# The triangular inverses of a delta-rule layer, moved from 64x64 units to compact 32x32 diagonal blocks with one corner step

## The chip, the core and the metric

One core of a Trainium2 chip runs one program that computes a four-layer network on 256 tokens of width 1024. The metric is the device time of one execution in microseconds, taken as the median of several runs. The engines are TensorE (PE, with its weight loads shown apart as PEld), VectorE (DVE), ScalarE (ACT), GpSimd (POOL) and the DMA queue of SyncE (SP). TensorE writes only to PSUM, which has eight banks of 512 float32 columns. VectorE and ScalarE carry results from PSUM to SBUF. VectorE also has a transpose that turns each 32x32 block of a tile in its place.

## What is computed

The network has an RG-LRU layer, a sparse attention layer, an RWKV-7 layer and a differential attention layer, each followed by a squared-ReLU MLP. The change touches only the recurrence of the third one:

```python
def _wkv7_scan(r, decay, k, v, a_in, b_in):
    def step(S, inp):
        r_t, w_t, k_t, v_t, a_t, b_t = inp
        sa = jnp.einsum('bhij,bhj->bhi', S, a_t)
        S = (S * w_t[:, :, None, :] + sa[..., None] * b_t[:, :, None, :]
             + v_t[..., None] * k_t[:, :, None, :])
        y_t = jnp.einsum('bhij,bhj->bhi', S, r_t)
        return S, y_t
```

There are 16 heads of width 64 and 256 tokens. The kernel cuts the tokens into four chunks of 64. Within a chunk the term with `sa` makes each token depend on the earlier ones, which is a triangular system: for each head and chunk it needs the inverse of a 64x64 matrix I - N, where N is strictly triangular. That is 16 heads x 4 chunks = 64 inverses. Everything is float32.

## The kernel before

The program is written out by hand, engine by engine, with semaphores. The order on an engine is the order of its code. `TURN`, `BANK` and `USE` (lines 86 to 196) give each use of a PSUM bank a number. `filled(q)` waits until TensorE has filled turn q, `taken(ins, q)` says that an engine has read it, `read_out` waits for that, and `open_bank` waits until a bank's last use has been read. `settle()` waits for the engine's own last instruction.

**Layout.** A unit is one chunk of one head pair: 64 columns on 128 partitions, head 0 on partitions 0 to 63 and head 1 on 64 to 127. There are 32 units, so one work buffer of 2048 columns holds all of them. They are handled in four groups i = 0..3 of 8 units.

**Inversion.** The inverse Y is built by doubling. At level l the diagonal blocks of size 2^(l+1) are completed from those of size 2^l: with L the part of N that joins two neighbouring blocks, the missing part of Y is Y L Y. VectorE first forms level 0 (lines 2544 and 2546) and turns it by 32x32 blocks into X (line 2552). For each level l = 1..5:

- GpSimd multiplies the Gram matrix by the level's mask into `RW_LM` (line 2796, four pieces), each as soon as TensorE is done with the piece of the level before.
- TensorE computes the product of the masked part with X for all four groups (`per_unit`, line 1054, turns `inv_t`), with one 64x64 matmul for each unit and head: 16 a group.
- ScalarE copies each bank to `RW_T1` (line 1829).
- TensorE multiplies this with the half of Y's columns that the level needs (`merged`, line 1198, turns `inv_xy`): again 16 a group.
- VectorE adds the result to Y (line 2575) and, but for the last level, turns the group's blocks into X (line 2552).

**Beside it.** In VectorE's queue, `v_gated` (line 2583) follows the four groups of level 1, and a quarter of splitting the weight tile `rw_o0` into a high and a low part (line 1996) follows the four groups of levels 1 to 4. ScalarE does the other part of that split (line 1443) and the scaling of `RW_G` (line 1836). Ahead of level 1 VectorE reads the `gram_k` banks (line 2566), and these banks are the ones that level 1 uses.

**After it.** TensorE goes on with the chunks of the recurrence (`heads`, line 1245): the first two products need nothing of the inversion, the third (turn `wkv_u`) reads Y.

Of the kernel before, what the change touches and what calls it, by code (L numbers as in the profile page):

```python
# [26 lines left out]
NT = T // CH  # L27
LEVELS = 6
# [36 lines left out]
for _n, _w in PARAM_COLS:  # L65
# [4 lines left out]
              ("mean_head", P), ("seg", T), ("gram_mask", 2 * CH), ("inv_mask", LEVELS * CH),  # L70
              ("diag", CH), ("center", CH)]
# [138 lines left out]
def build(nc, weights, params, consts, rows, heads, t5, x_in, out):  # L210
# [8 lines left out]
    with ctx:  # L219
# [79 lines left out]
        def units(i):  # L299
            return work[:, i, :].rearrange("p (c n t) -> p c n t", c=NC, n=NT)  # L300

# [3 lines left out]
        rw_gb = work[:, 8:10, :].rearrange("p a f -> p (a f)").rearrange("p (c n t) -> p c n t", c=NC, n=NT)  # L305
        rw_s = work[:, RW_X, 0:512].rearrange("p (c i) -> p c i", c=NC)
# [59 lines left out]
        def half(i):  # L366
            return slice(64 * i, 64 * i + 64)
# [83 lines left out]
        def _(pe):  # L451
# [736 lines left out]
            def merged(q, l, c0):  # L1188

                open_bank(q)  # L1190
                s = 1 << l
                for c in (c0, c0 + 1):
                    for tc in range(NT):
                        for hf in range(2):
                            at = ((c - c0) * NT + tc) * 32
                            cols = rw_y[half(hf), c, tc, :].rearrange("p (b a s) -> p b a s", a=2, s=s)[:, :, 1, :]
                            got = psum[half(hf), BANK[q], at:at + 32].rearrange("p (b s) -> p b s", s=s)
                            last = mm(got, units(RW_T1)[half(hf), c, tc, :], cols, start=True, stop=True)  # L1198
# [29 lines left out]
            for tc in range(NT):  # L1228
# [194 lines left out]
        def _(act):  # L1423
# [401 lines left out]
            for l in range(1, LEVELS):  # L1825
                for i in range(4):
                    q = TURN[("inv_t", l)] + i
                    filled(q)
                    taken(A(buf(RW_T1)[:, i * 512:i * 512 + 512], bank(q), ACT.Copy), q)
                if l < 5:  # L1830
                    split("rw_o0", [l - 1])
                if l > 1:
                    act.wait_ge(sig("v_gated"), 1)
                    for c in (2 * l - 4, 2 * l - 3):
                        g = chunks(RW_G)[:, c, :]
                        done(A(g, g, ACT.Copy, scale=col("lnx_g", c)), "g_scaled")

# [139 lines left out]
        def _(dve):  # L1977
# [561 lines left out]
            y_u = units_of(RW_Y)  # L2539
            gb_u = work[:, 8:10, :].rearrange("p a f -> p (a f)").rearrange("p (u a t) -> p u a t", a=2, t=CH)  # L2540
            for c in range(NC):
                read_out(dve, TURN["gram_b"] + c)
            filled(TURN["bt"] + 3)
            step(V.tensor_tensor(y_u, gb_u[:, :, 0, :], view(cst("inv_mask"), [[0, 32], [1, CH]]), ALU.mult))
            settle()
            done(V.tensor_tensor(y_u, y_u, view(cst("diag"), [[0, 32], [1, CH]]), ALU.add), "inv_first")  # L2546
            settle()

            def turn_blocks(i):

                f = slice(512 * i, 512 * i + 512)
                done(V.transpose(buf(RW_X)[:, f], buf(RW_Y)[:, f]), "inv_turned")
# [174 lines left out]
        def _(pool):  # L2727
# [58 lines left out]
            gb_u = work[:, 8:10, :].rearrange("p a f -> p (a f)").rearrange("p (u a t) -> p u a t", a=2, t=CH)  # L2786
            lm = work[:, RW_LM, :].rearrange("p (u t) -> p u t", t=CH)
            pool.wait_ge(sig("inv_first"), 1)
            for l in range(1, LEVELS):
                m = cst("inv_mask")[:, l * CH:l * CH + CH]  # L2790
                for i in range(4):
# [4 lines left out]
                    nc.gpsimd.tensor_tensor(lm[:, u, :], gb_u[:, u, 0, :], view(m, [[0, 8], [1, CH]]),  # L2796
# [45 lines left out]
def _consts():  # L2842
# [7 lines left out]
    for hf in range(2):  # L2850
        for th in range(2):
            for j in range(8):
# [10 lines left out]
    c["inv_mask"] = np.concatenate([(s < t) & (s >> (l + 1) == t >> (l + 1)) & (s >> l != t >> l)  # L2863
                                    for l in range(LEVELS)], 1)
# [96 lines left out]
```

## Time and profile before

| | |
|---|---|
| median of 3 runs | 1300.0 us (1299.5 to 1301.41) |
| span of the profiled execution | 1299.6 us, so it stands 0.4 us under the median |
| TensorE matmul busy | 1269.2 us (98%), 10,054 instructions |
| TensorE weight loads busy | 1098.1 us (84%), 10,059 instructions |
| VectorE busy | 894.2 us (69%) |
| ScalarE busy | 679.4 us (52%) |
| GpSimd busy | 83.8 us (6%) |
| chain that ended last | PE 83%, DVE 9%, ACT 6% |

Busy shares of the whole span say little of the 40 us that the change touches. A stretch is read from the timeline, which lists instructions in order with their count, length and what ended the idle time before them, and from the chain that ended last. A matmul row of the timeline gives the time from the first start to the last end of its instructions, so its length over its count is nearly the pace at which they start. A float32 matmul of the program on plain operands runs as two weight loads and two matmuls, so it counts twice in the trace (the 64 of a level are x128 there, less a record or two that the profiler lost); a transpose counts once. Each weight load and each matmul is an instruction that TensorE's queue has to bring in.

### The profile page before, as it was taken

To read this page: it belongs to the slowest core of one execution; us is meant where nothing else is said; L and a number is where in the kernel's file an instruction comes from. 1 tells how busy PE (TensorE), PEld (TensorE's weight loads), DVE (VectorE), ACT (ScalarE), POOL (GpSimd) and SP (SyncE) were. 2 spreads that over 40 slices of the span, in tenths; PEclk is the share of its full clock that TensorE was granted. 3 is DMA by queue.
4 is the path that set the end of the run, shared out by engine and by line. 5 is a ranking of instruction groups with operands and counts; after the bars stand their busy time and mean duration, and the time that the engine had idled before them with its cause. 6 is when DMAs were issued, how large, how long until landed. Compare 5 with 4: busy or idle time off the path is not lost.

```text
span 1299.6 us, 23670 instructions
## 1 busy us (share of the span) xinstructions
PE 1269.2 (98%) x10054; PEld 1098.1 (84%) x10059; DVE 894.2 (69%) x1467; ACT 679.4 (52%) x1228; POOL 83.8 (6%) x103
## 2 busy tenths in 40 slices
PE   9999999999999999999999999999999999999997
PEld 6978888889967888888898997888897987788886
DVE  6886666674685666656898848666668366766666
ACT  6874444463584454544663434444455477445452
POOL 3000500000060000000001600000000000000000
PEclk9999999999999999999999999999999999999999
DMA  9445454544412555553443003654555441455550
GB/s 351 159 184 200 184 190 184 188 188 166 165 62 81 200 195 194 194 195 130 164 161 131 5 36 114 219 193 188 195 194 194 176 161 61 187 194 194 195 194 33
DMA packets 17496, 214.45 MB, mean 165 GB/s; under 512 B 1960, under 2 KB 2128, under 8 KB 4720
## 3 DMA queue, kind: packets, MB, share of 16 engines
q1 hardware_dynamic: 15888, 205.43, 41.9%
q0 software_dynamic: 1504, 7.52, 1.6%
q8 instruction: 80, 1.31, 0.4%
q14 instruction: 24, 0.20, 0.0%
HBM read 211.87 MB, written 1.06 MB: 164 GB/s over the span
## 4 chain that ended last, share of the span: by engine, by line
PE 83%; DVE 9%; ACT 6%; issue 1%; DMA 1%; SPq 0%; DVEq 0%; ACTq 0%
PE psum L696 25%; PE psum L670 14%; PE psum L676 7%; PE psum L486 4%; PE psum L487 4%; PE psum L488 4%; DVE w_low L1996 3%; ACT w_high L1443 2%; PE psum L1054 2%; PE psum L1198 1%; PE psum L585 1%; PE psum L1245 1%; PE psum L1373 1%; PE psum L581 1%; PE psum L577 1%; PE psum L1069 1%
## 5 line engine op out<-in xcount | busy, mean ns | idle before, releaser
L1996 DVE TENSOR_TENSOR w_low<-ring,w_high 128x1024 fp32r<-128x1024 f32 x372 | 443.4, 1227 | 188.5 <-ACT w_high L1443 188.5
L1443 ACT ACTIVATE w_high<-ring 128x1024 fp32r<-128x1024 f32 x372 | 372.7, 1048 | 139.7 <-PE psum L696 105.4
L696 PE MATMUL psum<-w_high,up_split 128*128 128x512 f32 x1024 | 287.6, 391 | 0.8 <-DVE up_split L2151 0.8
L696 PEld LDWEIGHTS psum<-w_high,up_split 128*128 128x128 f32 x1024 | 190.3, 188 | 40.5 <-issue 2.7
L670 PE MATMUL psum<-act_split,w_high 128*128 128x512 f32 x768 | 191.6, 391 | 0.0
L696 PE MATMUL psum<-w_low,up_split 128*128 128x512 f32 x512 | 163.2, 390 | 0.0
L670 PEld LDWEIGHTS psum<-act_split,w_high 128*128 128x128 f32 x768 | 139.6, 189 | 26.0
L1544 ACT ACTIVATE up_split<-work 128x256 fp32r<-128x256 f32 x112 | 46.8, 418 | 159.4 <-DVE work L2144 148.8
L486 PE MATMUL psum<-act_split,w_high 128*128 128x256 f32 x448 | 129.1, 288 | 0.3 <-DVE act_split L2162 0.3
L487 PE MATMUL psum<-act_split,w_high 128*128 128x256 f32 x448 | 126.7, 283 | 0.0
L488 PE MATMUL psum<-act_split,w_low 128*128 128x256 f32 x448 | 126.7, 283 | 0.0
L696 PEld LDWEIGHTS psum<-w_low,up_split 128*128 128x128 f32 x512 | 96.1, 188 | 19.9
L676 PEld LDWEIGHTS psum<-act_split,w_low 128*128 128x128 f32 x768 | 104.8, 190 | 7.5
L676 PE MATMUL psum<-act_split,w_low 128*128 128x256 f32 x768 | 107.1, 282 | 0.0
L486 PEld LDWEIGHTS psum<-act_split,w_high 128*128 128x128 f32 x448 | 85.8, 191 | 3.9 <-issue 3.0
L487 PEld LDWEIGHTS psum<-act_split,w_high 128*128 128x128 f32 x448 | 85.9, 192 | 0.2
L488 PEld LDWEIGHTS psum<-act_split,w_low 128*128 128x128 f32 x448 | 85.8, 192 | 0.0
L2151 DVE TENSOR_TENSOR up_split<-work,up_split 128x256 fp32r<-128x256 f32 x112 | 47.7, 426 | 54.2 <-ACT up_split L1544 54.2
L1540 ACT ACTIVATE work<-psum 128x256 f32<-128x256 f32 x96 | 35.8, 373 | 41.7 <-PE psum L676 39.5
L2142 DVE TENSOR_TENSOR work<-psum,work 128x256 f32<-128x256 f32 x96 | 40.2, 419 | 19.3 <-ACT work L1540 19.3
L2796 POOL TENSOR_TENSOR work<-work,con 128x512 f32<-128x512 f32 x20 | 25.9, 1317 | 291.4 <-DVE work L2546 280.0
L2732 POOL DMA_DIRECT2D work<-rows x8 | 4.6, 574 | 620.6 <-DVE x L2042 338.9
(360 smaller groups left out, 1873.7 us busy)
## 6 DMA issues: line engine op xcount, KB each, us to landing
ring<-weights SPq DMA_DIRECT2D x95, 2048.0 KB, 7.5
work<-rows POOLq DMA_DIRECT2D x4, 1024.0 KB, 5.1
ring<-weights SPq DMA_DIRECT2D x4, 512.0 KB, 8.4
work<-rows POOLq DMA_DIRECT2D x4, 512.0 KB, 5.4
x<-x_in SPq DMA_DIRECT2D x2, 512.0 KB, 4.7
work<-t_bias POOLq DMA_DIRECT2D x1, 1024.0 KB, 8.4
out<-x SPq DMA_DIRECT2D x4, 256.0 KB, 2.1
con<-consts SPq DMA_DIRECT2D x1, 576.0 KB, 22.0
```

Of the source, the lines that this page charges most:

```text
L486: mm(out, w_hi, x_hi, start=start, stop=False)
L487: mm(out, w_hi, x_lo, start=False, stop=False)
L488: return mm(out, w_lo, x_hi, start=False, stop=stop)
L670: mm(bank(q), w_hi[:, at:at + P], act_split[:, k, :, :].rearrange("p s t -> p (s t)"), start=(k == 0), stop=False, skip_group_check=True)
L676: last = mm(bank(q, T), w_lo[:, at:at + P], act_split[:, k, 0, :], start=False, stop=(k == NC - 1), skip_group_check=True)
L696: last = mm(bank(acc[(th, n)]), up_split[:, m, a, P * th:P * th + P], w[:, f], start=start and i == 0, stop=stop and i == len(pairs) - 1, ...
L1443: A(high[:, HIGH_SLOT[name], f], ring[:, n % RING, f], ACT.Copy).then_inc(weights_high, 1)
L1540: A(up_part[:, m, :], bank(q)[:, T:2 * T], ACT.Copy).then_inc(sig("up_cross"), 1)
L1544: A(up_split[:, m, 0, :], up_sq[:, m, :], ACT.Copy).then_inc(sig("up_high"), 1)
L1996: V.tensor_tensor(low[:, n % RING, f], ring[:, n % RING, f], high[:, HIGH_SLOT[name], f].bitcast(f32), ALU.subtract).then_inc(weights_spli ...
L2142: taken(V.tensor_tensor(up_part[:, m, :], bank(q, T), up_part[:, m, :], ALU.add), q)
L2151: V.tensor_tensor(up_split[:, m, 1, :], up_sq[:, m, :], up_split[:, m, 0, :].bitcast(f32), ALU.subtract).then_inc(sig("up_split"), 1)
```

## The change

The two 32x32 diagonal blocks of each 64x64 matrix are inverted by themselves, and the corner that joins them is made in a last step. A 64x64 unit on 64 partitions becomes one 32x32 block on each group of 32 partitions, so a unit has 32 columns instead of 64, and a buffer of all units 1024 instead of 2048.

- The two blocks are gathered into `inv_m` by two VectorE instructions with a column of ones on the first or the last 32 partitions of a half (`upper`); the level-0 mask and the identity follow on 1024 columns.
- Levels 1 to 4 are as before on the compact blocks: `masked_product` and the new `merged` use four 32x32 matmuls a unit, on the four diagonal tiles of the array, where there were two of 64x64.
- Level 5 is new. `corner_product` multiplies the corner of the Gram matrix with X (two 32x32 matmuls a unit), ScalarE copies it, and `corners` computes the corner of the inverse and also moves the second diagonal block to the partitions' wide layout by an identity (four matmuls a unit). ScalarE copies this into the right half of `y_wide`, and VectorE writes the left half (`inv_wide`). GpSimd masks nothing for it, and VectorE adds nothing.
- The wait of VectorE for the `bt` transposes ahead of level 0 goes, since Y no longer lies in the buffer that they read.

```diff
-            for l in range(1, LEVELS):
+            def masked_product(q, i):
+                open_bank(q)
+                for n in range(8):
+                    for b in range(4):
+                        last = mm(psum[block(b), BANK[q], QB * n:QB * n + QB], inv_lm[block(b), 8 * i + n, :],
+                                  inv_x[block(b), 8 * i + n, :], start=True, stop=True)
+                last.then_inc(bank_filled, 1)
...
+                for n in range(8):
+                    for b in range(4):
+                        cols = inv_y[block(b), 8 * i + n, :].rearrange("p (b a s) -> p b a s", a=2, s=s)[:, :, 1, :]
+                        got = psum[block(b), BANK[q], 16 * n:16 * n + 16].rearrange("p (b s) -> p b s", s=s)
+                        last = mm(got, inv_t[block(b), 8 * i + n, :], cols, start=True, stop=True)
...
+            def corner_product(q, i):
+                open_bank(q)
+                for n in range(8):
+                    for b in (0, 2):
+                        last = mm(psum[block(b + 1), BANK[q], QB * n:QB * n + QB], gb_u[block(b), 8 * i + n, 0, QB:CH],
+                                  inv_x[block(b), 8 * i + n, :], start=True, stop=True)
+                last.then_inc(bank_filled, 1)
+            def corners(q, i):
+                open_bank(q)
+                for n in range(8):
+                    got = psum[:, BANK[q], QB * n:QB * n + QB]
+                    for b in (0, 2):
+                        y = inv_y[block(b + 1), 8 * i + n, :]
+                        mm(got[block(b), :], inv_t[block(b + 1), 8 * i + n, :], y, start=True, stop=True)
+                        last = mm(got[block(b + 1), :], cst("eye")[block(b + 1), :], y, start=True, stop=True)
+                last.then_inc(bank_filled, 1)
+            for l in range(1, LEVELS - 1):
                 for i in range(4):
                     pe.wait_ge(sig("inv_masked"), 4 * (l - 1) + i + 1)
                     pe.wait_ge(sig("inv_turned"), 4 * (l - 1) + i + 1)
-                    per_unit(TURN[("inv_t", l)] + i, 2 * i, lambda hf, c, tc: (
-                        units(RW_LM)[hf, c, tc, :], units(RW_X)[hf, c, tc, :]), CH)
+                    masked_product(TURN[("inv_t", l)] + i, i)
                 for i in range(4):
                     read_out(pe, TURN[("inv_t", l)] + i)
-                    merged(TURN[("inv_xy", l)] + i, l, 2 * i)
+                    merged(TURN[("inv_xy", l)] + i, l, i)
+            l = LEVELS - 1
+            for i in range(4):
+                pe.wait_ge(sig("inv_turned"), 4 * (l - 1) + i + 1)
+                corner_product(TURN[("inv_t", l)] + i, i)
+            for i in range(4):
+                read_out(pe, TURN[("inv_t", l)] + i)
+                corners(TURN[("inv_xy", l)] + i, i)
...
                 if tc == 0:
+                    pe.wait_ge(sig("inv_wide"), 4)
...
+            for i in range(4):
+                q = TURN[("inv_xy", LEVELS - 1)] + i
+                filled(q)
+                taken(A(y_wide[:, 8 * i:8 * i + 8, QB:CH], bank2(q)[:, 0, :].rearrange("p (u t) -> p u t", t=QB),
+                        ACT.Copy), q)
...
-            filled(TURN["bt"] + 3)
-            step(V.tensor_tensor(y_u, gb_u[:, :, 0, :], view(cst("inv_mask"), [[0, 32], [1, CH]]), ALU.mult))
+            first_rows, last_rows = cst("upper")[:, 0:1], cst("upper")[:, 1:2]
+            step(V.tensor_scalar(inv_m, gb_u[:, :, 0, 0:QB], first_rows, None, ALU.mult))
             settle()
-            done(V.tensor_tensor(y_u, y_u, view(cst("diag"), [[0, 32], [1, CH]]), ALU.add), "inv_first")
+            done(V.scalar_tensor_tensor(inv_m, gb_u[:, :, 0, QB:CH], last_rows, inv_m, ALU.mult, ALU.add), "inv_first")
             settle()
+            step(V.tensor_tensor(inv_y, inv_m, view(cst("inv_mask"), [[0, 32], [1, QB]]), ALU.mult))
+            settle()
+            step(V.tensor_tensor(inv_y, inv_y, view(cst("eye"), [[0, 32], [1, QB]]), ALU.add))
...
+                    if l == LEVELS - 1:
+                        u = slice(8 * i, 8 * i + 8)
+                        done(V.tensor_scalar(y_wide[:, u, 0:QB], inv_y[:, u, :], first_rows, None, ALU.mult), "inv_wide")
+                        continue
...
-                    cols = y_u[:, 8 * i:8 * i + 8, :].rearrange("p u (b a s) -> p (u b) a s", a=2, s=s)[:, :, 1, :]
-                    taken(V.tensor_tensor(cols, cols, bank(q, 256).rearrange("p (b s) -> p b s", s=s), ALU.add), q)
-                    if l < LEVELS - 1:
-                        settle()
-                        turn_blocks(i)
+                    cols = inv_y[:, 8 * i:8 * i + 8, :].rearrange("p u (b a s) -> p (u b) a s", a=2, s=s)[:, :, 1, :]
+                    taken(V.tensor_tensor(cols, cols, bank(q, 128).rearrange("p (b s) -> p b s", s=s), ALU.add), q)
+                    settle()
+                    turn_blocks(i)
...
-            for l in range(1, LEVELS):
-                m = cst("inv_mask")[:, l * CH:l * CH + CH]
+            for l in range(1, LEVELS - 1):
+                m = cst("inv_mask")[:, l * QB:l * QB + QB]
```

TensorE's order at the inversion before: the products with the masked part are L1054, those with Y are L1198, and L1245 is the recurrence.

```order
L1127 MATMUL psum<-work 64x128 x64
L1054 MATMUL psum<-work 64x64 x64
L1198 MATMUL psum<-work 64x32 x64
L1054 MATMUL psum<-work 64x64 x64
L1198 MATMUL psum<-work 64x32 x64
```

These are the program's matmuls, each twice in the trace; five such pairs of rows L1054 and L1198 stand there: 5 x 128 = 640. The same place now (L1202 `masked_product`, L1214 `merged`, L1222 `corner_product`, L1233 and L1234 `corners`):

```order
L1133 MATMUL psum<-work 64x128 x64
L1202 MATMUL psum<-work 32x32 x128
L1214 MATMUL psum<-work 32x16 x128
L1222 MATMUL psum<-work 32x32 x64
L1233 MATMUL psum<-work 32x32
L1234 MATMUL psum<-work,con 32x32
```

Four pairs of L1202 and L1214 stand there, then L1222, then 64 matmuls each of L1233 and L1234 in turn: 4 x 256 + 64 + 128 = 1216 matmuls against 640.

VectorE's order around level 1 before: L2566 reads the `gram_k` banks, L2575 adds, L2552 turns blocks, L2583 is `v_gated`, L1996 the split of weights.

```order
L2544 TENSOR_TENSOR work<-work,con 128x2048
L2546 TENSOR_TENSOR work<-work,con 128x2048
L2552 STREAM_TRANSPOSE work<-work 128x512 x4
L2561 SCALAR_TENSOR_TENSOR work<-psum,work 128x512 x4
L2566 TENSOR_TENSOR work<-psum,con 128x4x128 x8
L2575 TENSOR_TENSOR work<-work,psum 128x128x2
L2552 STREAM_TRANSPOSE work<-work 128x512
L2583 TENSOR_TENSOR work<-work 128x2048
L1996 TENSOR_TENSOR w_low<-ring,w_high 128x1024
L2575 TENSOR_TENSOR work<-work,psum 128x64x4
```

And now, with the add L2631, the turn L2604, `v_gated` L2638 and the split L2045:

```order
L2592 TENSOR_SCALAR work<-work,con 128x1024
L2594 SCALAR_TENSOR_TENSOR work<-work,con 128x1024
L2596 TENSOR_TENSOR work<-work,con 128x1024
L2598 TENSOR_TENSOR work<-work,con 128x1024
L2604 STREAM_TRANSPOSE work<-work 128x256 x4
L2613 SCALAR_TENSOR_TENSOR work<-psum,work 128x512 x4
L2618 TENSOR_TENSOR work<-psum,con 128x4x128 x8
L2631 TENSOR_TENSOR work<-work,psum 128x64x2
L2604 STREAM_TRANSPOSE work<-work 128x256
L2638 TENSOR_TENSOR work<-work 128x2048
L2045 TENSOR_TENSOR w_low<-ring,w_high 128x1024
L2631 TENSOR_TENSOR work<-work,psum 128x32x4
```

The queue keeps its order. Each add and each turn has half the elements, while `v_gated` and the split stay whole and in their places between the levels.

## Rows read from the trace of the kernel before

**Rows 1.** Timeline, 695 to 775 us: start, length, engine, line, operation, count, idle before.

```profile
705.93 2.14 PE L1160 MATMUL psum<-con,work 64*64 64x64 f32 x128 [0.76 <-ACT work L1818]
...
712.19 4.05 PE L1054 MATMUL psum<-work 64*64 64x64 f32 x127
...
716.11 3.83 PE L1198 MATMUL psum<-work 64*64 64x32 f32 x125
```

**Rows 2.** The chain that ended last, 680 to 800 and 730 to 752 us: start, length, what.

```profile
712.40 3.81 PE psum L1054 x127
...
733.01 0.16 issue
733.17 2.64 PE psum L1198 x85
735.81 1.25 PE psum L1054 x41
737.06 0.23 issue
737.29 2.70 PE psum L1054 x86
...
740.07 3.65 PE psum L1198 x124
...
743.77 1.08 PE psum L1054 x36
744.85 0.24 issue
...
751.86 0.38 issue
752.25 11.19 PE psum L1245 x372
```

**Rows 3.** Timeline, 695 to 775 us, VectorE alone.

```profile
710.56 4.87 DVE L2566 TENSOR_TENSOR work<-psum,con 128x512 f32<-128x512 f32 x8
...
717.24 0.42 DVE L2575 TENSOR_TENSOR work<-work,psum 128x256 f32<-128x256 f32 x1 [1.81 <-PE psum L1198]
717.69 0.71 DVE L2552 STREAM_TRANSPOSE work<-work 128x512 f32<-128x512 f32 x1
718.33 0.38 DVE L2575 TENSOR_TENSOR work<-work,psum 128x256 f32<-128x256 f32 x1
...
721.49 2.79 DVE L2583 TENSOR_TENSOR work<-work 128x2048 f32<-128x2048 f32 x1
...
724.20 2.11 DVE L1996 TENSOR_TENSOR w_low<-ring,w_high 128x1024 fp32r<-128x1024 f32 x1
...
730.47 1.47 DVE L1996 TENSOR_TENSOR w_low<-ring,w_high 128x1024 fp32r<-128x1024 f32 x1
```

**Rows 4.** Timeline, 326.4 to 327.2 us, in the sparse attention layer.

```profile
326.73 0.47 PE L863 MATMUL psum<-par,small 64*15 64x64 f32 x32
```

**Rows 5.** Groups by line and shape, VectorE and ScalarE, whole span.

```profile
L2348 DVE CUSTOM_DVE_ANT_0 work<-psum,work 128x256 f32<-128x256 f32 x32 | 11.6, 419 | 1.7 <-PE psum L919 1.6
L2348 DVE CUSTOM_DVE_ANT_0 work<-psum,work 128x128 f32<-128x128 f32 x32 | 7.4, 287 | 2.3 <-PE psum L919 2.2
L2508 DVE TENSOR_TENSOR work<-work 128x2048 f32<-128x2048 f32 x1 | 2.3, 2293 | 0.1
L1540 ACT ACTIVATE work<-psum 128x256 f32<-128x256 f32 x96 | 35.8, 373 | 41.7 <-PE psum L676 39.5
```

**Rows 6.** The page, part 3: DMA queue, kind: packets, MB, share of 16 engines.

```profile
q8 instruction: 80, 1.31, 0.4%
```

**Rows 7.** Busy time by stretch: PE, PEld, DVE, ACT, POOL, granted clock, DMA share, GB/s.

```profile
716.00:724.00 8.00, 8.00 (x277) 7.92 (x274) 6.62 (x9) 3.38 (x6) 4.65 (x4) 1.00 0.02 4
...
1070.00:1072.00 2.00, 0.95 (x8) 0.83 (x8) 1.35 (x2) 2.00 (x7) 0.00 (x0) 1.00 0.98 418
...
1074.00:1076.00 2.00, 2.00 (x7) 1.46 (x6) 1.97 (x11) 1.49 (x5) 0.00 (x0) 0.52 0.00 0
```

More of the change, by code:

```diff
@@ L27 @@
 NT = T // CH
+QB = 32
 LEVELS = 6
@@ L69 @@
 CONST_COLS = [("dist", T), ("cmp_bias", 2 * 2 * 8 * NCMP), ("cmp_valid", 2), ("ident", P), ("mean_d", P),
-              ("mean_head", P), ("seg", T), ("gram_mask", 2 * CH), ("inv_mask", LEVELS * CH),
-              ("diag", CH), ("center", CH)]
+              ("mean_head", P), ("seg", T), ("gram_mask", 2 * CH), ("inv_mask", (LEVELS - 1) * QB),
+              ("eye", QB), ("upper", 2), ("diag", CH), ("center", CH)]
 CONST_AT, NCONST = {}, 0
@@ L305, in build @@
         rw_gb = work[:, 8:10, :].rearrange("p a f -> p (a f)").rearrange("p (c n t) -> p c n t", c=NC, n=NT)
+        gb_u = work[:, 8:10, :].rearrange("p a f -> p (a f)").rearrange("p (u a t) -> p u a t", a=2, t=CH)
+        inv_x, inv_m = (work[:, RW_X, 1024 * i:1024 * i + 1024].rearrange("p (u t) -> p u t", t=QB) for i in range(2))
+        inv_lm, inv_y = (work[:, RW_LM, 1024 * i:1024 * i + 1024].rearrange("p (u t) -> p u t", t=QB) for i in range(2))
+        inv_t = work[:, RW_T1, 0:1024].rearrange("p (u t) -> p u t", t=QB)
+        y_wide = work[:, RW_Y, :].rearrange("p (u t) -> p u t", t=CH)
         rw_s = work[:, RW_X, 0:512].rearrange("p (c i) -> p c i", c=NC)
@@ L1186, in _, with block @@
                 across(TURN["gram_k"] + i, i, gram(RW_KD), 2 * CH)
-            def merged(q, l, c0):
+            def block(b):
+                return slice(QB * b, QB * b + QB)
+            def masked_product(q, i):
[5 more added lines that the diff above has]
+                last.then_inc(bank_filled, 1)
@@ L1190, in merged @@
+            def merged(q, l, i):
                 open_bank(q)
                 s = 1 << l
[L1192 to L1198, printed above, removed]
@@ L1828, in _ @@
                     filled(q)
-                    taken(A(buf(RW_T1)[:, i * 512:i * 512 + 512], bank(q), ACT.Copy), q)
+                    taken(A(inv_t[:, 8 * i:8 * i + 8, :], bank2(q)[:, 0, :].rearrange("p (u t) -> p u t", t=QB),
+                            ACT.Copy), q)
                 if l < 5:
@@ L1836, in _ @@
                         done(A(g, g, ACT.Copy, scale=col("lnx_g", c)), "g_scaled")
+            for i in range(4):
+                q = TURN[("inv_xy", LEVELS - 1)] + i
+                filled(q)
+                taken(A(y_wide[:, 8 * i:8 * i + 8, QB:CH], bank2(q)[:, 0, :].rearrange("p (u t) -> p u t", t=QB),
+                        ACT.Copy), q)
             def heads_high(tc):
@@ L2795, in _ @@
                     u = slice(8 * i, 8 * i + 8)
-                    nc.gpsimd.tensor_tensor(lm[:, u, :], gb_u[:, u, 0, :], view(m, [[0, 8], [1, CH]]),
+                    nc.gpsimd.tensor_tensor(inv_lm[:, u, :], inv_m[:, u, :], view(m, [[0, 8], [1, QB]]),
                                             ALU.mult).then_inc(sig("inv_masked"), 1)
@@ L2862, in _consts @@
     c["gram_mask"] = np.concatenate([s < t, s <= t], 1)
-    c["inv_mask"] = np.concatenate([(s < t) & (s >> (l + 1) == t >> (l + 1)) & (s >> l != t >> l)
-                                    for l in range(LEVELS)], 1)
+    s32, t32 = p % QB, np.arange(QB)[None, :]
+    c["inv_mask"] = np.concatenate([(s32 < t32) & (s32 >> (l + 1) == t32 >> (l + 1)) & (s32 >> l != t32 >> l)
+                                    for l in range(LEVELS - 1)], 1)
+    c["eye"] = s32 == t32
+    c["upper"] = np.concatenate([s < QB, s >= QB], 1)
     c["diag"] = s == t
```

10 lines of the change are left out of this document (4 added, 6 removed).

## The prediction

> **What bounds the kernel now.** I read the chain of waits first, then the timeline of the stretch it points to, then the pace at which matmuls start, and last what that pace rests on. The chain of the third layer runs on TensorE: the first level of the inversion from 712.40, and so on until the fifth level ends at 751.86 and the recurrence starts at 752.25 [rows 2]. The inversion is 39.7 us of it (712.2 to 751.9). TensorE is busy 8.00 of 8.00 us at clock 1.00 there, with DMA at 0.02 [rows 7], and VectorE idles 1.81 us before its first add [rows 3]: it follows.
>
> *The pace.* 127 products with 64 moving columns take 4.05 us, 125 with 32 take 3.83 [rows 1]. One lasts 0.22, so the starts are (4.05 - 0.22) / 126 = 30.4 ns apart, and 29.1 for half the columns: moving data don't set it. Both go round two tiles of the array, one for each head. L1160 goes round four 64x64 tiles: (2.14 - 0.22) / 127 = 15.1 ns [rows 1]. So a tile takes 60 ns for a weight load of 64 columns and its matmul, and tiles share that time: 60 / 2, 60 / 4. L863, with weights of 15 columns on four tiles a row half, has starts (0.47 - 0.22) / 31 = 8.1 ns apart for 32 of them [rows 4], the closest in the trace.
>
> *The stops.* In the chain, TensorE stops for "issue" at 733.01, 737.06 and 744.85 [rows 2]. Between the first two stand 85 + 41 = 126 matmuls, between the second and third 86 + 124 + 36 = 246, twice that: one stop for each 126 matmuls with their loads, some 252 instructions. 
>
> - 2304 pairs go round four tiles. If 32 columns of weights load in half the time of 64, a tile takes some 32 ns and the pace is 8 ns, which L863 shows to be possible. Its upper end is the 15.1 of L1160. I take 8: 18.4 us. The 128 pairs of `corner_product` go round two tiles, 15 ns, 1.9 us. Together 20.3.
> - 2432 / 126 = 19 packets end in the inversion, where 10 do now. What is queued lasts a quarter as long at 4 ns an instruction as at 15, so the halts show almost whole: 19 x 0.65 = 12.4.
> - Waits of the instruction stream, two a bank, were under the same cover; I add 0.5.
>
> The sum is 33.2 in place of 39.7: 6.5 us less.
>
> Two rules of the Trainium skill pull apart here. "Runtime: NRT & Kernel Launch", section "Instruction fetch mechanics", has instructions brought in blocks of 256, with the cost of crossing a block mostly hidden. The trace agrees on the size (252) and shows three halts that aren't hidden. "TensorE: Matmul & The Clock Gate", section "Wait — 56ns, not 53.3ns?", has starts never closer than about 25 ns. The rows' 15.1 and 8.1 disagree.
>
> **VectorE's part**, summed to see whether it is covered. It has read the last `gram_k` bank at 710.56 + 4.87 = 715.43 [rows 3], as now. An add and a turn start at 717.24, 717.69 and the next add at 718.33: 1.09 a group. Half the columns of a PSUM operand save 419 - 287 = 132 ns [rows 5], so the add goes from 0.40 to 0.27. At 2293 ns for 2048 columns [rows 5], 256 fewer columns save some 0.27 of the turn's 0.64: 0.37. A group is 0.66 with a gap of 0.02, between 0.53 (all halves) and 1.09 (nothing saved); four are 2.6. The weight splits between the levels are 2.11 and 1.47 in two of its rows now [rows 3], beside GpSimd's masks, whose pieces get half as long; I take 1.4. `v_gated` is 2.79; 2.29 for the same size alone; I take 2.5. A level is 4.0 us, the first 6.5 with `v_gated`. TensorE's is 33.2 x 512 / 2432 = 7.0. So VectorE is hidden in all of them, and would bound at 715.4 + 4 x 2.6 + 2.5 + 3 x 1.4 = 732.5 for the last turn, plus 2 us for the last level and the hand-overs between levels: 735, 17 us early, if TensorE cost nothing.
>
> **What costs nothing.** The four instructions ahead of level 1 (1024 columns, about half of 2.29 each, in place of two of 2.29) lie before 712.2 while TensorE does `kt`, `vt` and `gram_k`, and VectorE then waits for `vt` anyway; so the wait for `bt` that goes gives nothing. Of the added waits, `inv_wide` holds TensorE before `wkv_u`, with the whole recurrence behind it. VectorE writes these four pieces after the fourth split, early by several us. ScalarE's four copies into `y_wide` (0.37 each [rows 5]) end 0.6 us after the last corner, beside 128 pairs of the recurrence (3.8 us at 30 ns) that need nothing of them. ScalarE's level (four copies of 0.37, a split, two scalings, some 3.5 us) is shorter than TensorE's. If any of these covers were gone it would cost 0.5 to 1.5 us, once.
>
> **After the inversion** all moves along: the DMA share of 0.02 says that the weight slots are full and wait for TensorE. The profiled span of 1299.6 becomes 1293.1; the median, 0.4 above it, 1293.5.
>
> **Rivals.**
>
> - *The halts stay hidden*, or are 0.3. Then TensorE needs 20 to 26 us and VectorE bounds at about 735: 1283 to 1287. For it: most halts are hidden now. Against: the queue that hides them runs out in a quarter of the time. The skill's "mostly hidden" would give this.
> - *A 32x32 tile is no faster than a 64x64 one*, which ends slower. The mechanism is a fixed time for a pair on a tile, or an issue of instructions that can't beat L1160's 15.1 ns, the best that the trace holds over more than 32 pairs. 2304 x 15.1 + 128 x 30.4 = 38.7 us, and the halts, part hidden at that pace, add 19 x 0.4 = 7.6: 46.3, so 6.6 slower, 1306.6. It decides from (39.7 - 12.9) / 2432 = 11.0 ns a pair on. L863 speaks against it, but its weights have 15 columns and it ends after 32.
> - *Four row tiles shut each other out* in their common PSUM bank. L1054 has two row tiles in one bank at full pace; no row has four. If the tiles took turns at 30 ns a pair, 2432 take 73 us: 1333. The skill's page "TensorEngine Tiling (Array Packing)", "Gotcha 1: PSUM Pressure", forbids different row tiles the same bank at the same time; L1054's pace shows no such wait. Its 25 ns a start, above, would be 61 us, an estimate of 1321.
> - *The clock falls.* A stretch in which TensorE was busy 0.95 of 2 us is followed by one at 0.52, the 1.2 GHz level [rows 7]. Here TensorE halts for a third of the time. At half clock a level's matmuls take twice as long and hide the halts: some 3 us for one or two such stretches, 1296.5.
> - *Something behind gives it back*: 1297 to 1300. Full slots speak against it.
>
> **How the numbers follow.** Forecast 0.58, with its own range of 1289 (halts of 0.45) to 1298.5 (halts of 0.9). Hidden halts 0.12. Tiles no faster 0.14. Shut out or 25 ns 0.05. Clock 0.07. Given back 0.04. The range of 1285 to 1303 takes in the forecast, the clock, and the near parts of the first two rivals. 0.2% (2.6 us) is what a measurement here can tell from no change. Faster: nearly all of the forecast, the hidden halts, half of the clock, 0.74. The same: 0.09. Slower: 0.17.
>
> **What would show it.** Runs of 32x32 matmuls 8 ns apart, broken about every 126 by idle "issue" of 0.4 to 0.7 us; 99 packets in the instruction queue in place of 80; VectorE waiting for TensorE in every level; the recurrence near 746. The forecast is wrong if the pace inside a run is 15 ns, if the breaks are short or longer than 1 us, or if VectorE no longer waits.

## The result, and the profile after

The changed kernel takes 1334.4 us (median of 4 runs, 1333.8 to 1338.0) against 1300.0: 34 us slower, a ratio of 1.0267 (95% interval 1.0253 to 1.0281). I had forecast 1293.5 and a range of 1285 to 1303. The profiled run took 1338.0, the longest of the four; its span is 1336.2, 36.6 more than the span before.

The page after, parts 3 and 4 (queue: packets, MB, share; share of the chain by engine):

```profile
q8 instruction: 89, 1.46, 0.4%
...
PE 79%; DVE 10%; ACT 5%; issue 3%; DMA 1%; SPq 0%; DVEq 0%; ACTq 0%
```

The chain of waits after, 712 to 735 us and further on (start, length, what), which answers to [rows 2]:

```profile
712.26 0.60 PE psum L1202 x45
712.87 0.86 issue
713.72 1.39 PE psum L1202 x100
715.12 2.54 issue
717.66 1.21 PE psum L1202 x57
...
718.91 0.69 PE psum L1214 x38
719.60 2.04 issue
721.63 1.92 PE psum L1214 x126
723.55 1.78 issue
725.33 1.20 PE psum L1214 x59
...
726.58 0.69 PE psum L1202 x38
727.27 1.48 issue
728.75 1.92 PE psum L1202 x127
730.68 1.50 issue
732.17 1.24 PE psum L1202 x76
...
771.13 0.91 PE psum L1222 x33
772.04 1.60 issue
773.65 2.50 PE psum L1222 x86
...
783.33 13.42 PE psum L1287 x371
```

TensorE runs some 127 matmuls with their loads (one block), stands for 1.5 to 2.5 us without waiting for anything the profile shows, and runs the next 127. The restarts at 717.66, 721.63, 725.33, 728.75, 732.17 go on in this way to 773.65, fifteen steps later: (773.65 - 717.66) / 15 = 3.73 us apart, none under 3.4 and none over 4.0. The inversion lasts from 712.26 to 783.33, 71.1 us in place of the 40.0 from 712.2 to 752.25 [rows 2]; that is 31.0 of the 36.6 us.

The DMA queue that brings the instructions moves with it. Its row for 712.26 to 783.33 us (packets, MB, share):

```profile
q8 instruction: 19, 0.31, 1.9%
```

By the trace these 19 packets start from 714.96 to 782.34 us, (782.34 - 714.96) / 18 = 3.74 us apart, and each restart of TensorE up to 773.65 comes 2.2 to 2.8 us after the start of one of them.

The windows after, which answer to [rows 7] (busy us of PE, PEld, DVE, ACT, POOL; granted clock; DMA share, GB/s):

```profile
712.00:716.00 4.00, 2.26 (x192) 1.86 (x182) 3.29 (x6) 1.01 (x3) 1.24 (x2) 1.00 0.02 4
716.00:720.00 4.00, 1.94 (x127) 1.83 (x127) 0.00 (x0) 1.41 (x3) 1.28 (x2) 0.65 0.02 4
720.00:730.00 10.00, 5.11 (x346) 4.87 (x350) 5.54 (x10) 0.68 (x2) 0.71 (x1) 0.50 0.02 5
...
782.00:792.00 10.00, 9.35 (x259) 9.24 (x252) 1.10 (x2) 2.10 (x5) 0.00 (x0) 0.66 0.02 5
```

From 720 to 730 us TensorE is busy for about half of the time, where it was busy for all of it, and its clock falls to 0.50 at 717.3 and is back at 789.0. The first runs, at full clock, have the pace I took from L863. The timeline after (start, length, engine, line, operation, count, idle before):

```profile
712.19 0.67 PE L1202 MATMUL psum<-work 32*32 32x32 f32 x54
713.72 1.39 PE L1202 MATMUL psum<-work 32*32 32x32 f32 x127 [0.86 <-issue]
...
721.63 1.92 PE L1214 MATMUL psum<-work 32*32 32x16 f32 x127 [2.04 <-issue]
...
815.12 0.39 PE L1287 MATMUL psum<-work 64*64 64x64 f32 x7 [2.37 <-issue]
```

(0.67 - 0.24) / 53 = 8.1 ns and (1.39 - 0.24) / 126 = 9.1 ns a pair; at half clock (1.92 - 0.24) / 126 = 13.3. The other 5.3 us are behind the inversion: from the recurrence's first matmul to the output projection it is 35.0 us (783.33 to 818.35) in place of 29.7 (752.25 to 781.94). Of these 2.2 are its first 372 matmuls, 13.42 in place of 11.19 [rows 2], the first 5.6 us of them at half clock.

### The profile page after: what moved, and what is told of

Its sections match the earlier page's. It is cut to its first block, busy times and chain, and to the rows that moved or that the text cites. A ratio compares the mean times of both kernels' runs of the same rounds, so it can differ in the third digit from the quotient of the medians.

```text
span 1336.2 us, 25976 instructions
## 1 busy us (share of the span) xinstructions
PE 1270.4 (95%) x11206; PEld 1097.8 (82%) x11211; DVE 885.7 (66%) x1469; ACT 676.4 (51%) x1232; POOL 71.2 (5%) x99
## 4 chain that ended last, share of the span: by engine, by line
PE 79%; DVE 10%; ACT 5%; issue 3%; DMA 1%; SPq 0%; DVEq 0%; ACTq 0%
PE psum L702 25%; PE psum L676 13%; PE psum L682 7%; PE psum L492 4%; PE psum L493 4%; PE psum L494 4%; DVE w_low L2045 3%; PE psum L1287 2%; ACT w_high L1486 2%; PE psum L591 1%; PE psum L587 1%; DMA ring<-weights 1%; PE psum L1214 1%; PE psum L1202 1%; PE psum L583 1%
## 5 line engine op out<-in xcount | busy, mean ns | idle before, releaser
L2045 DVE TENSOR_TENSOR w_low<-ring,w_high 128x1024 fp32r<-128x1024 f32 x372 | 442.0, 1224 | 188.1 <-ACT w_high L1486 188.1
L2191 DVE TENSOR_TENSOR work<-psum,work 128x256 f32<-128x256 f32 x96 | 40.2, 419 | 19.3 <-ACT work L1583 19.3
L2193 DVE SCALAR_TENSOR_TENSOR work<-work 128x256 f32<-128x256 f32 x96 | 40.8, 426 | 3.3
```

What stands on the lines that cost most here:

```text
L2045: V.tensor_tensor(low[:, n % RING, f], ring[:, n % RING, f], high[:, HIGH_SLOT[name], f].bitcast(f32), ALU.subtract).then_inc(weights_spli ...
L2191: taken(V.tensor_tensor(up_part[:, m, :], bank(q, T), up_part[:, m, :], ALU.add), q)
L2193: V.scalar_tensor_tensor(up_sq[:, m, :], up_part[:, m, :], 0.0, up_part[:, m, :], ALU.max, ALU.mult).then_inc(sig("up_squared"), 1)
```

## The experiments

The theory was now: **TensorE gets its instructions in blocks of some 252, and a block can't follow the last one by less than 3.4 to 4.0 us, however short its work is.** That makes 14.8 ns an instruction, 29.6 for a load and its matmul: the kernel before, at 30.4, ran just above it. The rivals: the stops belong to the banks and their waits, the tiles' own time, the clock. The runs came on several chips, on which the kernel before stood at 1300 to 1304 us; each ratio is to its runs on the same chip.

**Half the instructions.** Every bank, wait and moved column stays.

```diff
-                for n in range(8):
+                for n in range(0, 8, 2):
-  last = mm(psum[block(b), BANK[q], QB * n:QB * n + QB], inv_lm[block(b), 8 * i + n, :],
-            inv_x[block(b), 8 * i + n, :], start=True, stop=True)
+  last = mm(psum[block(b), BANK[q], QB * n:QB * (n + 2)], inv_lm[block(b), 8 * i + n, :],
+            inv_x[block(b), 8 * i + n:8 * i + n + 2, :], start=True, stop=True)
... (merged, corner_product and corners alike)
```

> The changed kernel with half of its inversion matmuls: each takes two units' moving columns with one unit's weights (64 or 32 columns in place of 32 or 16), so every bank, wait and moved column stays and 1216 matmuls become 608; the inverse is of wrong numbers. Supply theory (TensorE gets its instructions in blocks of about 252 and can't get one more often than each 3.4 to 4.0 us, whatever they are): 1216 pairs are 9.7 blocks in place of 19.3, so the inversion falls from 70 to about 36 us, the blocks still 3.4 to 4.0 us apart, and the kernel from 1334 to 1297 to 1301. Rival, the stops belong to banks and their waits (40 of them, all still there): only the matmuls' own 36 us halve, 1316. Rival, the tiles' time with moving columns sets it: the columns are all still there, 1330 or more.

1299.8 us, ratio 0.9996 (0.9982 to 1.0009). The inversion takes 38.3 us (711.3 to 749.6; I had expected 36), with 80 packets in the instruction queue. Its chain still stops between blocks, fewer of them:

```profile
714.65 2.31 issue
716.96 1.23 PE psum L1215 x74
...
749.56 12.95 PE psum L1288 x372
```

The loss went with the instructions; banks and columns, all still there, cost nothing that shows.

**Twice the columns in the same instructions.**

```diff
-  last = mm(psum[block(b), BANK[q], QB * n:QB * n + QB], inv_lm[block(b), 8 * i + n, :],
-            inv_x[block(b), 8 * i + n, :], start=True, stop=True)
+  k = 1 + (n < 7)
+  last = mm(psum[block(b), BANK[q], QB * n:QB * (n + k)], inv_lm[block(b), 8 * i + n, :],
+            inv_x[block(b), 8 * i + n:8 * i + n + k, :], start=True, stop=True)
```

> The changed kernel with twice the moving columns (64 in place of 32) in seven of eight matmuls of the masked product, the same number of instructions, the same result. Supply theory: no change, within 2.5 us of 1334.4, since the tiles work in time in which TensorE otherwise stands; the bursts of about 127 matmuls get longer (1.9 us to 2.5 or 3.4) and the stops behind them shorter by as much. If the longer work holds the clock up, the recurrence gets 2 us back. Rival, TensorE's own time bounds and the stops are something fixed: 1024 pairs get up to 12 ns longer at half clock, +6 to +12 us, 1340 to 1346.

1331.9 us, 1.0239 (1.0219 to 1.0260): no longer. The median is 2.5 us shorter, which the intervals of the two ratios can't tell from nothing. The chain of this kernel in a stretch at half clock shows why:

```profile
727.86 3.42 PE psum L1203 x119
731.27 0.62 issue
...
735.38 1.90 PE psum L1215 x127
737.28 1.80 issue
```

A block of the widened product works 3.42 us and stops 0.62; one of the narrow second product works 1.90 and stops 1.80. The stop is what is left of the 3.7 to 4.0, not a price of its own.

**Four tiles in the kernel before.** The product goes over two banks at once, crosswise:

```diff
-  last = mm(psum[half(hf), BANK[q], at:at + width], lhsT, rhs, start=True, stop=True)
+  last = mm(psum[half((hf + tc) % 2), BANK[q + tc % 2], at:at + width], lhsT, rhs, start=True, stop=True)
```

> The kernel before, 64x64 matmuls in the same number, but going round four tiles of the array in place of two (every second unit's output goes to the other half of the other bank; the inverse is of wrong numbers). By the rows of before four tiles go at 15.1 ns a pair in place of 30.4. Supply theory: 1280 pairs are 10.2 blocks at 3.4 to 4.0 us, 35 to 41 us in place of 39.7: TensorE stands idle half of the time and the kernel stays within 1296 to 1303, the lower clock after idle time in the upper part. Rival (the kernel before is bound by its tiles, and a block's end costs about 0.65 us, as I predicted): 1280 x 15.1 + 10 x 0.65 = 26 us, VectorE then bounds at 28 to 32, 1288 to 1292.

1303.0 us, 1.0015 (1.0001 to 1.0028). Nothing is gained over the kernel before, though a round over four tiles could take half the time. I read from its chain that TensorE waited 16 us for GpSimd's masks, and ran it again with half the masks:

```diff
-  units(RW_LM)[hf, c, tc, :], units(RW_X)[hf, c, tc, :]), CH)
+  units(RW_LM)[hf, c // 2 * 2, tc, :], units(RW_X)[hf, c, tc, :]), CH)
-  u = slice(8 * i, 8 * i + 8)
+  u = slice(8 * i, 8 * i + 4)
```

> e3_four_tiles with GpSimd masking only half of the units (the matmuls of every second chunk use the weights of the one before it): in e3_four_tiles TensorE waited 16 us for GpSimd's masks, which the pairs of banks made late, so it did not tell the theories apart. Supply theory: 10.2 blocks, still 35 to 41 us and 1296 to 1303, now with stops for issue in place of the waits for GpSimd. Rival (tiles bound before): 26 us and VectorE's pace, 1286 to 1292.

1303.0 us, 1.0013 (1.0000 to 1.0026), the same. My reading of the chain was wrong: GpSimd's share in it is time that the chain spent on GpSimd, while TensorE still had queued work. The waits of the first run say it, 708 to 752 us (waiting line, for whom, us, times, longest):

```profile
PE psum L1210 <- issue: 8.1, 12, 1.4
...
PE psum L1210 <- POOL work L2815: 2.7, 2, 1.4
```

Two of the four windows of the second run, those with the fewest matmuls:

```profile
712.00:722.00 10.00, 7.02 (x309) 6.59 (x312) 7.31 (x13) 4.17 (x7) 3.51 (x5) 0.85 0.02 5
...
742.00:752.00 10.00, 6.36 (x282) 5.97 (x284) 5.35 (x10) 3.35 (x7) 0.00 (x0) 0.88 0.01 3
```

TensorE idles for 3.0 and 3.6 of 10 us and still starts no more than 309 and 282 matmuls; the kernel before starts 277 in 8 us, busy for all 8 [rows 7]. Over all four windows, 712 to 752 us, it is 1263 matmuls with TensorE idle for 10.8 of 40 us, and 9.1 us of its waits there are for issue. Its clock is down for a part of each, but an idle engine isn't bound by it. The 10 instruction packets of this stretch start 4.03 us apart on the mean, not 3.73, so a few of the 40 us are other waits, and not every stop for issue is the end of a block. Still, the 1280 pairs are 10.2 blocks, 38 us at 3.73, and the kernel before took 40.0: it stood at both limits at once, or within 2 us of it.

**More instructions with next to no work**, first in the kernel before, then in the changed one:

```diff
+  spare = psum[CH * hf:CH * hf + 1, BANK[q], 256 + at // 32:257 + at // 32]
+  last = mm(spare, units(RW_T1)[half(hf), c, tc, 0:1], units(RW_T1)[half(hf), c, tc, 0:1], start=True, stop=True)
```

> The kernel before with one matmul more behind each of the 320 of the second product, of one weight column and one moving column into a spare column of the bank; the result is as before. Supply theory: 640 pairs, 1280 instructions, 5.1 blocks more at 3.4 to 4.0 us: the inversion gets 17 to 20 us longer, 1317 to 1322, with a lower clock behind it in the upper part. Rival, tiles' time: a pair of one column takes at most the 8.1 ns of the fastest row: 640 x 4 to 8 ns, +2.6 to +5.2 us, 1303 to 1305.

1429.5 us, 1.0992 (1.0975 to 1.1008): 128 us more, outside both theories. The timeline of this kernel:

```profile
716.59 0.30 PE L1198 MATMUL psum<-work 64*64 64x32 f32 x2
716.82 0.19 PE L1200 MATMUL psum<-work 64*1 64x1 f32 x2
716.93 0.30 PE L1198 MATMUL psum<-work 64*64 64x32 f32 x2
```

The one-column weights have another tile shape, and now nothing overlaps: a matmul and its small neighbour take 0.345 us where the matmul alone took 0.06, and 0.467 at half clock. 320 times 0.28 to 0.41 are 90 to 130 us. I read it as the price of a change of tile shape, not of the supply. The next one keeps the shape, with one moving column too, and shows no such price.

```diff
+  last = mm(psum[block(b), BANK[q], 256 + n:257 + n], inv_t[block(b), 8 * i + n, :],
+            inv_t[block(b), 8 * i + n, 0:1], start=True, stop=True)
```

> The changed kernel with 512 matmuls more, one behind each of the second product, of the same 32x32 weights and one moving column into a spare column; the same tile shape, so no change of the array's mode (such changes are what made e4_tiny 129 us slower: 0.11 to 0.12 us at each). Supply theory: 1024 pairs are 8.1 blocks at 3.4 to 4.0 us, +28 to +32 us, 1361 to 1367, while TensorE has idle time enough for them. Rival, TensorE's own time: 8 ns each at full clock and 15 at half, +8 to +15 us, or nothing if they fall into the stops: 1334 to 1349.

1361.8 us, 1.0466 (1.0443 to 1.0488): 27 more than the changed kernel, a little under the 28 to 32 of the supply theory and well over the 15 that tiles could take; 97 packets, eight more. The inversion alone takes 101.0 us (710.91 to 811.93), 30 more than in the changed kernel; the stretch behind it is shorter (30.2 us in place of 35.0). Its chain:

```profile
735.64 1.93 PE psum L1202 x127
737.57 2.05 issue
739.62 1.23 PE psum L1202 x76
```

From the restart at 720.28 to the one at 795.00 it is 20 steps, 3.74 us on the mean, 3.3 at the least and 4.0 at the most.

**A quarter of the instructions**, as in the first experiment:

```diff
-                for n in range(8):
+                for n in range(0, 8, 4):
...
+            inv_x[block(b), 8 * i + n:8 * i + n + 4, :], start=True, stop=True)
```

> The changed kernel with a quarter of its inversion matmuls (each takes four units' moving columns with one unit's weights; the inverse is of wrong numbers). It tests the sum for VectorE and the supply theory's limit. Supply theory: 608 pairs are 4.8 blocks, 18 us; VectorE then bounds, by the prediction's sum at 735 against 752 of the kernel before: 1283 to 1288, and VectorE no longer waits for matmuls in every level. If something else between the engines bounds (hand-overs, GpSimd's masks), 1289 to 1296. Stops of banks (already refuted by e1_half): 1306.

1286.4 us, 0.9884 (0.9863 to 0.9904). The timeline of VectorE:

```profile
715.53 0.28 DVE L2632 TENSOR_TENSOR work<-work,psum 128x128 f32<-128x128 f32 x1
715.84 0.45 DVE L2605 STREAM_TRANSPOSE work<-work 128x256 f32<-128x256 f32 x1
716.21 0.25 DVE L2632 TENSOR_TENSOR work<-work,psum 128x128 f32<-128x128 f32 x1
...
732.57 0.45 DVE L2605 STREAM_TRANSPOSE work<-work 128x256 f32<-128x256 f32 x1
```

Groups are 0.66 us apart and the last turn ends at 733.0; I had 0.66 and 732.5. The recurrence starts at 735.5. VectorE waits for TensorE only once by then, for 0.50 us. So the compact blocks are worth 17 us to VectorE, as summed, of which 15 show in the time (1286.4 against 1301.2), and the changed kernel can't cash them.

**The clock held up** by two 512-column bfloat16 matmuls ahead of each bank:

```diff
                 open_bank(q)
+                idle(q, 2)
```

> The changed kernel with two 512-column bfloat16 matmuls ahead of each of the 40 banks of the inversion (the real ones overwrite them): 17 us of work in TensorE's idle time, to hold the clock up. Supply theory: 160 instructions are 0.6 block, +2.3 us; if the clock stays up the recurrence takes 11.2 again in place of 13.4 us for its first 372 matmuls, -2.2, and the slow first matmuls behind the recurrence go: 1328 to 1337. The stops stay, 3.4 to 4.0 us from block to block. Rival, the clock's fall is what costs in the inversion: the pace of 15.1 ns becomes 8 for 2304 pairs, -16 us, 1318 to 1322. Or the clock doesn't come up, 1335 to 1340.

1344.0 us, 1.0322 (1.0300 to 1.0344), worse, and outside all that I had expected, the supply theory's 1328 to 1337 too. The clock was up for 30 of the inversion's 80 us. The chain of one bank at half clock (L468 are the added matmuls) shows where the time went:

```profile
740.69 0.34 issue
741.03 0.63 PE psum L468
741.66 0.98 PE psum L1216 x64
```

One bank of 64 pairs takes 1.95 us, of which TensorE is idle 0.34 at the change to the wide matmuls. Two banks, 128 pairs or a block, take 3.9 us: the added work fills the 3.73 and goes beyond. So it does not say what the clock is worth.

**Fewer instructions for the same product: bfloat16**, in the kernel before:

```diff
-  last = mm(got, units(RW_T1)[half(hf), c, tc, :], cols, start=True, stop=True)
+  last = mm(got, h_t[half(hf), c * NT + tc, :], cols, start=True, stop=True)
+  step(V.tensor_copy(h_y[:, u, :], y_u[:, u, :]))
... (h_x, h_y, h_t, h_lm are bfloat16)
```

> The kernel before, 64x64 matmuls on two tiles as it had them, with the inversion's four matmul operands in bfloat16 (a copy of y in bfloat16 is made by VectorE ahead of each turn, and y itself stays float32): the program's 640 matmuls then run as one load and one matmul each in place of two and two, and the inverse is of lower precision. Supply theory: 1280 instructions are 5.1 blocks, 19 us in place of 37.6, tiles 640 x 30 = 19 us, so both limits are gone and VectorE bounds: a group of add, copy and turn about 1.3 us, a level 5.2 with the split's 1.8 = 7.0, four of them 28, v_gated 2.8: the inversion ends about 747 to 749 in place of 752, 1294 to 1297. If the copies and turns of 2-byte data are much cheaper, 1287 to 1293. Rival, a float32 matmul's second half costs nothing (a weight load in the shadow of the other tile's): no change but VectorE's copies, 1300 to 1303.

1304.4 us, 1.0036 (1.0017 to 1.0056). The block limit is gone (from 716.77 to 751.01 us the instruction packets start 7.8 to 10.3 us apart), but VectorE's group of add, copy and turn takes 1.52 us, not my 1.3, and a level 7.6 to 8.0 (it is busy for 9.6 to 9.8 of each 10 us from 712 to 752, so it bounds now); the clock is at half meanwhile, and the recurrence's 372 matmuls take 13.2 us. Slower on VectorE means no gain, so I joined it with the compact blocks.

**Compact blocks on VectorE, few instructions on TensorE.**

```diff
+  last = mm(psum[half(hf), BANK[q], QB * n:QB * n + QB], inv_lms[(l - 1) % 2][half(hf), 8 * i + n, :],
+            inv_x[half(hf), 8 * i + n, :], start=True, stop=True)
+  A(inv_t[:, u, 0:QB], got, ACT.Copy, scale=cst("upper")[:, 0:1])
+  taken(A(inv_t[:, u, QB:CH], got, ACT.Copy, scale=cst("upper")[:, 1:2]), q)
```

> A version that follows from the others: VectorE's compact 32-column blocks of the changed kernel, but TensorE's 64x64 matmuls on two tiles as before, 640 in all (the weights are the whole 64x64 unit with zeros off the blocks, written by GpSimd's mask and by two scaled copies of ScalarE; the moving operand is the compact one, 32 or 16 columns), and the operands in bfloat16, so each matmul is one load and one matmul; GpSimd's masks have two buffers. Supply theory: 5.1 blocks are 19 us, tiles 640 x 30.4 = 19.5 us, e5_quarter and e9_bf16 show that VectorE bounds then: a group of add and turn 0.66, a level 2.6 + 1.8 for the split, four of them and v_gated 20.2 from 716.5: the inversion ends at 736 to 740 in place of 752 and the kernel takes 1285 to 1291, less than before. TensorE works most of that time, so the clock should hold. Rival, hand-overs between the engines (ScalarE's two copies, GpSimd's 1.1 us masks) bound at 6 us a level or more: 1293 to 1300.

**1288.5 us, 0.9912 (0.9898 to 0.9925): faster than both kernels by 12 and 46 us**, at bfloat16's precision in the inversion. The recurrence starts at 737.3. From 724.96 to there the chain is ScalarE's, its copies of 0.36 us, the split and the scalings (11 us of GpSimd's masks come before). Is the gain that of the compact work or of the number of instructions? The same in float32:

```diff
-        inv_lms = [small_units(f"h_lm{i}", RW_LM, 4096 * i, CH) for i in range(2)]
+        inv_lms = [work[:, RW_LM, :].rearrange("p (u t) -> p u t", t=CH)] * 2
... (inv_x, inv_y, inv_t alike)
```

> e10_compact_bf16 in float32 (one buffer for GpSimd's masks, as before): the same 640 matmuls of 64x64 tiles and the same compact VectorE work, but two loads and two matmuls each. It tells whether e10's gain is from VectorE's compact work or from the number of instructions. Supply theory: 1280 pairs are 10.2 blocks, 37 to 38 us, and the tiles' 640 x 2 x 30.4 ns = 38.9: TensorE bounds again as in the kernel before, 1298 to 1302. Rival, VectorE's part bounded before: 1288 to 1292, as e10.

1326.1 us, 1.0172 (1.0148 to 1.0195), which neither theory had. Its chain:

```profile
716.16 5.59 PE psum L1215 x125
721.86 6.84 PE psum L1201 x127
728.70 6.71 PE psum L1215 x125
```

and a window of it:

```profile
722.00:732.00 10.00, 10.00 (x193) 10.00 (x192) 5.58 (x6) 5.09 (x11) 6.25 (x4) 0.50 0.01 3
```

From 722 to 762 us TensorE is never short of instructions and never idle, and its clock is at half from 717.4 for 61 us: a pair takes 6.84 / 127 = 53.9 ns in place of 30. The matmuls are as many and the weights as wide as in the kernel before, but the moving columns are 32 and 16 where those were 64 and 32. This led to the last question, answered by giving only the columns back:

```diff
+  k = 1 + (n < 7)
-  last = mm(psum[half(hf), BANK[q], QB * n:QB * n + QB], inv_lms[(l - 1) % 2][half(hf), 8 * i + n, :],
-            inv_x[half(hf), 8 * i + n, :], start=True, stop=True)
+  last = mm(psum[half(hf), BANK[q], QB * n:QB * (n + k)], inv_lms[(l - 1) % 2][half(hf), 8 * i + n, :],
+            inv_x[half(hf), 8 * i + n:8 * i + n + k, :], start=True, stop=True)
... (merged alike, 32 columns in place of 16)
```

> e11_compact_f32 with two units' moving columns in seven of eight matmuls (64 and 32 in place of 32 and 16; the second half is overwritten by the next matmul, the result stays). Clock theory: TensorE falls to half clock when its matmuls have few moving columns, even if it is busy all the time; with the columns of the kernel before the clock stays at 1.00, the pace returns to 30 ns a pair from 54, and the kernel to 1298 to 1302. Rival (something else of e11 slows the tiles, or the clock falls all the same): 1322 or more.

1302.1 us, 1.0008 (0.9994 to 1.0021). A window of it beside the one above:

```profile
722.00:732.00 10.00, 9.81 (x326) 9.69 (x325) 7.60 (x11) 6.71 (x16) 9.04 (x6) 1.00 0.02 5
```

The same matmuls with more columns run at full clock, 326 in 10 us in place of 193. So the compact blocks' short moving operands cost some 21 us (1.0172 less 1.0008) through the clock alone where TensorE bounds, and with the columns back the compact VectorE work is worth nothing in float32: blocks and tiles still bound TensorE. The gain of the bfloat16 version needs its half as many instructions. These are 5 blocks in place of 10 and half the tiles' time as well; no run tells these two apart. The same columns in that version:

> e10_compact_bf16 with the same doubled moving columns. VectorE and the masks bound it, so the inversion should stay as it is, within 1 us; if the clock stays up longer, the recurrence's first 372 matmuls take 11.2 again in place of 12.1 us: 1285 to 1289. If TensorE's idle time alone makes the clock fall, 1287 to 1290.

1288.2 us, 0.9899 (0.9882 to 0.9915), no different. The clock still falls for 24 us, in this kernel with TensorE busy 6.01 of 10 us in the worst window. Its chain is on GpSimd's masks from 714.07 to 724.00 and on ScalarE alone from 726.50 to the recurrence at 738.64, with VectorE's part beside it: a slower TensorE has room there. I had expected VectorE and the masks to bound.

## Why the prediction was wrong

1. **The step that failed is the halt at a packet's end**, "I bound it by 0.3 and 0.9 us and take 0.65", and with it the term 19 x 0.65 = 12.4. I took the halt for a fixed price that a queue hides in part. It is what remains of a fixed spacing: 3.73 us from block to block less the time the block's work takes. At the old pace 126 x 30.4 ns = 3.83 us leave nothing over, at 9 ns 2.5 us (seen once, 2.54), at 13.3 ns 1.5 to 2.1. The term should have been the whole: 2432 / 126 = 19.3 blocks x 3.73 = 72 us, where 71.1 were measured. The 3.73 is from the same run; e7_more tests it apart, 3456 / 126 = 27.4 blocks, 102 us, where 101.0 were measured. That tiles go faster cancels out of it. The prediction's own sign of being wrong, breaks longer than 1 us, came true. Why a block can't follow sooner is not shown by any run. e1_half, e2_wide, e7_more and the two on four tiles each moved one of the two quantities, and only the instructions moved the time.
2. **The pace inside a run** was right: 8 ns forecast, 8.1 to 9.1 seen at full clock. It did not matter.
3. **The count of blocks** was right at 19 in the inversion, and 19 packets start in it. The 99 packets I named for the queue were a slip: 1152 more pairs / 126 is nine, and the page shows 89.
4. **VectorE**, "hidden in all of them" and bounding at 735 only if TensorE cost nothing, was right: in e5_quarter, with TensorE's part small, the recurrence starts at 735.5.
5. **The clock**: I gave it 0.07 and 3 us. It fell for 71.7 us. Within the inversion that cost nothing that shows (e2_wide had the clock up for parts of it and took 70.6 us); behind it the recurrence's first 372 matmuls lost 2.2. The other 3.1 us behind the inversion stay open. A stop of 2.37 us ahead of 815.12 is among them; the instruction packet before it starts at 812.71, 6.63 us after the last one, just behind a stretch with the DMA share at 0.89 (809 to 812 us). No run tests whether that load held it up. And e7_more, with the same matmuls there, needed 30.2 us for the whole stretch.
6. **The rivals.** "Shut each other out" gave 1333, near the result, by a mechanism that the runs exclude: the four tiles of a bank run 8 to 9 ns apart, and not 25 either. "A tile is no faster" is excluded by the same rows. "The halts stay hidden", for which I cited the Trainium skill, "Runtime: NRT & Kernel Launch", section "Instruction fetch mechanics", is the reverse of what happened. The section says that instructions are dispatched more slowly than they are filled in, which hides the fetch. The trace disagrees for small matmuls: 127 pairs, 254 instructions, ran in 1.39 us, 5.5 ns each, and were filled in at 3.73 us / 252 = 14.8 ns each.

A small slip has no bearing: by its own terms the forecast's range of 1289 to 1298.5 comes to 1289.7 and 1298.2.

It could have been seen ahead. [rows 2] show three stops, 4.05 and 7.79 us apart, one and two blocks, and a block's 126 pairs at 30.4 ns are 3.83: a kernel that stops for issue though its tiles are busy all the time is near the rate at which it gets instructions. I read the stop's length and not the distance between stops.

## What to carry to other kernels

## What was not expected of the hardware

- When TensorE waits for them, blocks of some 252 instructions follow each other at 3.4 to 4.0 us, 3.73 on the mean of 15, in the changed kernel, and at 3.3 to 4.0, 3.74 on the mean of 20, in e7_more. After the one block that ran at full clock (713.72 to 717.66 in the changed kernel) it is 3.94, within the same bounds.
- With 64x64 weights and 32 and 16 moving columns in float32 the clock was at 0.50 in a window with TensorE busy 10.00 of 10.00 us (e11_compact_f32); with 64 and 32 columns it was at 1.00, busy 9.81 (e12_columns).
- Matmuls of 64x64 and 64x1 tiles in turn (e4_tiny) take 0.28 us more at full clock than the 0.06 of the first alone.
